# Sample-state visits: the outer products move from GpSimd to TensorE, six low weights from VectorE to GpSimd

## What is computed

```python
u = _rmsnorm(x, norm_w) @ w_in        # z, x/B/C, dt, q, k, v, z_att, g_ssd, g_att
# one decoding step, per sequence b, head h, channel p, state n (E heads share B and C):
h_new = exp(dt*A) * h + (dt * x)[p] * B[n]       # written out: state_ssm
y     = sum_n(C[n] * h_new) + d_skip * x
y     = rmsnorm_by_group(y * silu(z)) * ssd_norm_w
br_ssd, br_att = y @ w_ssd_br, o @ w_att_br
mix   = sigmoid(g_ssd) * br_ssd + sigmoid(g_att) * br_att
out   = x + mix @ w_out
```

## Time and profile before

| | |
|---|---|
| median of 3 runs | 1071.72 us (1069.91 to 1073.2) |
| profiled execution | 1071.67 us, of which the span of the instructions is 1069.9 us |
| busy: PE, DVE, ACT, POOL | 998.1, 714.5, 534.0, 270.4 us |
| mean granted clock of TensorE | 0.986 |
| DMA | 198.00 MB, mean 185 GB/s |

### The profile page before, as it was taken

One profiled execution on the slowest core, in us unless ns is written; L12 is line 12 of the kernel. 1 busy time (PEld: TensorE's weight loads), 2 busy tenths in 40 slices (PEclk: granted clock), 3 DMA queues, 4 the chain that ended last, 5 costly groups with the idle time before them and its releaser, 6 DMA issues.

```text
span 1069.9 us, 21735 instructions
## 1 busy us (share of the span) xinstructions
PE 998.1 (93%) x8420; PEld 934.2 (87%) x8420; DVE 714.5 (67%) x1135; ACT 534.0 (50%) x1289; POOL 270.4 (25%) x339
## 2 busy tenths in 40 slices
PE   3998889999999998999999999999999987799998
PEld 2998878999999886399988988988999987799998
DVE  6857577576777387677878878888845577634332
ACT  5435556566574655045555555555545658212110
POOL 0222122242332111011321321421314898100000
PEclk9999999999999999999999999999999999799999
DMA  9361533345541257563463643543679997422221
GB/s 385 122 244 62 240 124 139 142 190 222 197 159 61 82 189 257 175 236 129 175 239 131 231 181 130 232 180 124 239 281 371 369 346 255 165 80 79 105 84 50
DMA packets 30261, 198.00 MB, mean 185 GB/s; under 512 B 4520, under 2 KB 6792, under 8 KB 20688
## 3 DMA queue, kind: packets, MB, share of 16 engines
q1 hardware_dynamic: 25664, 183.09, 45.1%
q0 software_dynamic: 4496, 13.54, 3.3%
HBM read 179.89 MB, written 104.70 MB: 266 GB/s over the span
## 4 chain that ended last, share of the span: by engine, by line
PE 63%; DVE 14%; ACT 10%; issue 7%; DMA 4%; POOL 1%; SPq 0%; ACTq 0%; DVEq 0%; POOLq 0%
PE bank L698 30%; PE bank L732 14%; PE bank L745 5%; DVE cacc L1715 4%; ACT wH L1283 3%; PE bank L921 1%; DMA slot<-in_state_ssm 1%; DVE yL L2146 1%; PE bank L821 1%; PE bank L861 1%; DMA out_tail<-tail 1%; PE bank L878 1%; PE bank L780 1%; PE bank L998 1%; DVE hst L2070 1%
## 5 line engine op out<-in xcount | busy, mean ns | idle before, releaser
L698 PE MATMUL bank<-xH,wH 128*128 128x260 f32 x976 | 204.2, 290 | 4.4 <-DVEq L1629 1.8
L698 PE MATMUL bank<-xH,wL 128*128 128x260 f32 x976 | 197.1, 283 | 0.0
L698 PE MATMUL bank<-xL,wH 128*128 128x260 f32 x976 | 196.5, 283 | 0.0
L1283 ACT CAST wH<-w_raw 128x2048 fp32r<-128x2048 f32 (+1 forms) x81 | 122.1, 1507 | 91.3 <-PE bank L698 83.5
L698 PEld LDWEIGHTS bank<-xH,wH 128*128 128x128 f32 x976 | 150.7, 189 | 14.6 <-issue 12.3
L698 PEld LDWEIGHTS bank<-xH,wL 128*128 128x128 f32 x976 | 150.9, 189 | 0.0
L698 PEld LDWEIGHTS bank<-xL,wH 128*128 128x128 f32 x976 | 150.8, 189 | 0.0
L732 PE MATMUL bank<-wH,xH 128*128 128x256 f32 x480 | 142.8, 298 | 7.7 <-DVE xL L1663 7.0
L732 PE MATMUL bank<-wL,xH 128*128 128x256 f32 x480 | 137.7, 287 | 0.0
L732 PE MATMUL bank<-wH,xL 128*128 128x256 f32 x480 | 137.3, 286 | 0.0
L1684 DVE TENSOR_TENSOR wL<-w_raw,wH 128x2048 fp32r<-128x2048 f32 (+1 forms) x45 | 104.7, 2327 | 48.0 <-ACT wH L1283 46.9
(11 more groups left out here) (298 smaller groups left out, 2122.4 us busy)
## 6 DMA issues: line engine op xcount, KB each, us to landing
w_raw<-in_weights SPq DMA_DIRECT2D x62, 1024.0 KB, 5.2
out_kvs<-in_cache SPq DMA_DIRECT2D x16, 2044.0 KB, 10.8
ring<-in_cache SPq DMA_DIRECT2D x48, 256.0 KB, 3.8
slot<-in_state_ssm SPq DMA_DIRECT2D x16, 512.0 KB, 6.3
out_ssm_s<-slot POOLq DMA_DIRECT2D x16, 512.0 KB, 5.7
out_kvs<-in_cache SPq DMA_DIRECT2D x8, 508.0 KB, 7.2
out_kvp<-st POOLq DMA_DIRECT2D x18, 128.0 KB, 3.7
out_kvp<-vv POOLq DMA_DIRECT2D x18, 128.0 KB, 2.1
```

Source lines behind the costliest of these rows:

```text
L698: mm = pe.matmul(bk[hf].tile[:, 0:HALF], wslot(w, i)[:, k, s * P:(s + 1) * P], x[:, k, hf * HALF:(hf + 1) * HALF], start=(k == 0 and n == ...
L1283: return nc.scalar.copy(out, in_)
```

## The change

**Outer products on TensorE.** B, C and dt\*x of the samples are split into high and low parts, laid out as (group, part, sequence) rows in `BC3` and `XD3`, and turned by TensorE ("srows": two 128x128 products ahead of the barrier; "sxturn": four behind it). VectorE spreads the turned B and C into `spreadB` and `spreadC`, where row k holds its values at its own sequence and zeros elsewhere (two instructions of 128x1024, in "sproducts"). With them "sgroup" is two fp32r products of 128x512 (16 rows deep, C only), and a new step "supdate" u forms the outer product of visit u in banks 6 and 7 with two fp32r products of 128x512 (24 rows deep). VectorE adds the two banks to the decayed state, and GpSimd only issues the store. "sbcopy", `Bsp` and `outer` are gone.

**Low weights.** `POOL_SPLITS` is now `("ga", "ba")`: for these six items GpSimd forms `wL` in one instruction, in "use" of the first unit of the item before. VectorE passes over them, and waits for the one before bs 0.

**Order.** "oparts" moves into beat 0, the loads of states 3 and 4 into beat 2 ("slate"), the y parts to the last four beats (2, 4, 5, 5 of them, ahead of "use"), "sampleparts" into the last beat ahead of its parts.

```diff
-POOL_SPLITS = ()
+POOL_SPLITS = ("ga", "ba")
...
+PARTS = (0, 2, 6, 11, UNITS)
...
-        if beat % PER_GROUP == 1 and beat < UNITS:
-            out.append(("sbcopy", beat // PER_GROUP))
+        if beat == 0:
+            out.append(("oparts",))
+        if beat == 2:
+            out.append(("slate",))
         if 0 < beat <= UNITS:
-            out.append(("sdecay", beat - 1))
+            out += [("sdecay", beat - 1), ("supdate", beat - 1)]
...
+        left = len(rest) - 1 - beat
+        if left == 0:
+            out.append(("sampleparts",))
+        if left < 4:
+            out += [("parts", u) for u in range(PARTS[3 - left], PARTS[4 - left])]
         out.append(use)
-        left = len(rest) - 1 - beat
-        if left <= 4:
-            out += [("parts", u) for u in range(4 * (4 - left), 4 * (5 - left)) if u < UNITS]
...
+                elif op == "supdate":
+
+                    u = a[0]
+                    g, k = divmod(u, PER_GROUP)
...
+                    lo, hi = 32 * g, 32 * g + 3 * B
+                    for half in range(2):
+                        bk = banks[6 + half]
+                        bk.take(pe, ("outer", u))
+                        pe.matmul(bk.tile[:, :], XT3[lo:hi, k, :],
+                                  spreadB[lo:hi, 4 * half:4 * half + 4, :].rearrange("k b n -> k (b n)"), start=True, stop=True)\
+                          .then_inc(bk.filled, 1)
...
+                elif op == "supdate":
 
                     u = a[0]
-                    g = u // PER_GROUP
-                    pool.wait_ge(S["b_spread_ready"], 2 * (g + 1))
...
-                    nc.gpsimd.tensor_tensor(outer[:, :, :], Bsp[:, :, :], XD[:, u, :].unsqueeze(2).to_broadcast([P, B, P]),
-                                            ALU.mult).then_inc(S["sample_outer_ready"], 1)
...
-                    nc.gpsimd.tensor_tensor(st_u[:, :, :], st_u[:, :, :], outer[:, :, :], ALU.add).then_inc(S["sample_state_ready"], 1)
                     pool.wait_ge(S["sample_state_ready"], u + 1)
-                    pool.dma_start(ssms_out[u], st_u[:, :, :]).then_inc(S[f"state_kept{u % SLOTS_S}"], 16)
+                    pool.dma_start(ssms_out[u], slots[u % SLOTS_S][:, :, :]).then_inc(S[f"state_kept{u % SLOTS_S}"], 16)
...
+                elif op == "supdate":
+
+                    u = a[0]
+                    st_u = slots[u % SLOTS_S]
+                    dve.wait_ge(S["sample_decayed"], u + 1)
+                    for half in range(2):
+                        bk = banks[6 + half]
+                        bk.full(dve, ("outer", u))
+                        mine = st_u[:, 4 * half:4 * half + 4, :]
+                        ins = TT(mine, mine, bk.tile[:, :].rearrange("p (c n) -> p c n", c=4), ALU.add)
+                        if half == 0:
+                            ch.link(ins)
+                            free(bk)
+                    ins.then_inc(S["sample_state_ready"], 1)
...
```

More of the change, by code:

```diff
@@ L1017, in _ @@
                     pe.wait_ge(S["cb_products_ready"], 1)
-                    banks[6].take(pe, ("cb",))
-                    pe.matmul(banks[6].tile[:, 0:GROUPS * B], ones[:, :], cbp[:, :, :].rearrange("p g b -> p (g b)"),
-                              start=True, stop=True).then_inc(banks[6].filled, 1)
+                    banks[7].take(pe, ("cb",))
+                    pe.matmul(banks[7].tile[:, 0:GROUPS * B], ones[:, :], cbp[:, :, :].rearrange("p g b -> p (g b)"),
+                              start=True, stop=True).then_inc(banks[7].filled, 1)
+                elif op == "srows":
+                    pe.wait_ge(S["sample_rows_ready"], 2)
+                    banks[7].take(pe, ("rows",))
+                    for q in range(2):
+                        mm = pe.matmul(banks[7].tile[:, q * P:(q + 1) * P],
+                                       BC3[:, q, :, :, :].rearrange("p g c b -> p (g c b)").bitcast(F32), ident, start=True, stop=True)
+                    mm.then_inc(banks[7].filled, 1)
+                elif op == "sxturn":
+                    pe.wait_ge(S["sample_xdt_ready"], 3)
+                    banks[6].take(pe, ("xdt",))
+                    for k in range(PER_GROUP):
+                        mm = pe.matmul(banks[6].tile[:, k * P:(k + 1) * P],
+                                       XD3[:, k, :, :, :].rearrange("p g c b -> p (g c b)").bitcast(F32), ident, start=True, stop=True)
+                    mm.then_inc(banks[6].filled, 1)
                 elif op == "sgroup":
@@ L1582, in _ @@
                     A(rs8[:, :, :], rs8[:, :, :], ACT.Exp, scale=-0.5).then_inc(S["sample_scale_ready"], 1)
+                elif op == "srowsplit":
+                    cp(oneR[:, :], ones[:, 0:1])
+                    act.wait_ge(S["bc_samples_kept"], GROUPS)
+                    cp(BC3[:, :, :, 0:4:2, :].rearrange("p q g c b -> p (q g) c b"),
+                       BCS[:, :, :, :].rearrange("p q g b -> p (q g) b").unsqueeze(2).to_broadcast([P, 2 * GROUPS, 2, B]))\
+                        .then_inc(S["sample_rows_ready"], 1)
+                elif op == "sproducts":
+                    act.wait_ge(S["sample_xdt_ready"], 1)
+                    for k in range(PER_GROUP):
+                        ins = cp(XD3[:, k, :, 0:2, :], XD[:, k:UNITS:PER_GROUP, :].unsqueeze(2).to_broadcast([P, GROUPS, 2, B]))
+                    ins.then_inc(S["sample_xdt_ready"], 1)
                 elif op == "oparts":
@@ L1585, in _ @@
                         cp(oH[:, hp, :], oT[:, hp, :]).then_inc(S["o_high_ready"], 1)
-                elif op == "sbcopy":
-                    g = a[0]
-                    if g > 0:
-                        act.wait_ge(S["sample_outer_ready"], PER_GROUP * g)
-                    for half in range(2):
-                        bk = banks[6 + half]
-                        bk.full(act, ("Bsp", g, half))
-                        cp(Bsp[:, 4 * half:4 * half + 4, :], bk.tile[:, :].rearrange("p (c n) -> p c n", c=4)).then_inc(S["b_spread_ready"], 1)
-                        act.wait_ge(S["b_spread_ready"], 2 * g + half + 1)
-                        free(bk)
+                elif op == "sxturn":
+                    banks[6].full(act, ("xdt",))
+                    cp(XT3[:, :, :], banks[6].tile[:, :].rearrange("p (k n) -> p k n", k=PER_GROUP)).then_inc(S["sample_xdt_turned"], 1)
+                    act.wait_ge(S["sample_xdt_turned"], 1)
+                    free(banks[6])
                 elif op == "sdecay":
@@ new lines, in _ @@
+                    banks[7].full(dve, ("rows",))
+                    for n, (q, dst) in enumerate(((1, spreadC), (0, spreadB))):
+                        TT(dst[:, :, :], banks[7].tile[:, q * P:(q + 1) * P].unsqueeze(1).to_broadcast([P, B, P]),
+                           place8[:, :].unsqueeze(2).to_broadcast([P, B, P]), ALU.mult).then_inc(S["sample_rows_ready"], 1)
+                        if n == 0:
+                            dve.wait_ge(S["sample_xdt_ready"], 2)
+                            for k in range(PER_GROUP):
+                                ins = TT(XD3[:, k, :, 2:4, :], XD[:, k:UNITS:PER_GROUP, :].unsqueeze(2).to_broadcast([P, GROUPS, 2, B]),
+                                         XD3[:, k, :, 0:2, :].bitcast(F32), ALU.subtract)
+                            ins.then_inc(S["sample_xdt_ready"], 1)
@@ L2106, in _ @@
+                    dve.wait_ge(S["sample_rows_ready"], 4)
+                    free(banks[7])
                 elif op == "sprep":
[L2107 to L2109 removed]
+                    banks[7].full(dve, ("cb",))
+                    ch.link(V.tensor_copy(cbd[:, :, :], banks[7].tile[:, 0:GROUPS * B].rearrange("p (g b) -> p g b", g=GROUPS)))
```

76 lines of the change are left out of this document (43 added, 33 removed).

## The result

The changed kernel takes 1087.03 us (median of 4 runs, 1084.84 to 1088.39) against 1072.2 (1069.91 to 1073.2) for the kernel before beside it: ratio 1.0126, 95% interval 1.01 to 1.0152. It is slower, by 14.8 us. The profiled execution has 1086.08 us, 1084.3 of them span.

What follows compares the result with a forecast made beforehand. The prediction took TensorE, state loads and, in the last four beats, VectorE to bound the stage in turn. "ba" 1 19.7 us behind and a tail of 21.6 us instead of 30.3 put 11.0 on 1071.67: 1082.7 us, range 1078 to 1088.

## What to carry over

When a cheap step moves to an idle engine, ask what it now waits behind on that engine, and which queue waits for it: here an idle GpSimd cost 15 us because its subtraction stood behind a store that waited for two other engines. Look at what a queue issues next to a late, small, urgent transfer: exchanging it with a 2 MB copy that nobody waits for was worth 15 us, nearly as much as undoing the move. Then look at what stands behind the copy now. And where a loop has two late links in series, removing either may give back the whole loss; test each alone before adding gains.
